# Dividing a third product of each channel group into quarters in a float32 hybrid trunk kernel on one core

## The chip, the core and the metric

The kernel runs on one core of a Trainium2 chip. TensorE multiplies, ScalarE and VectorE cut every float32 operand into a high and a low part, GpSimd forms sums of weights, and SyncE issues most of the transfers. The metric is the time of one execution in microseconds; the median of several runs counts.

## What is computed

One layer of a trunk with two token mixers. All of it starts with one wide projection of the normalised input, 1024 tokens by 1024 channels:

```
h = rmsnorm(x, norm_g)
proj = h @ w_in
b_a, c_a, x_a, z_a, q, k, v, z_b, g_a, g_b = split(proj)
y_a = short_conv_branch(b_a, c_a, x_a, z_a, ...)      # silu(z) * B * conv3(C * x), then a projection
y_b = retention_branch(q, k, v, z_b, w_b_out)         # rotary q and k, decayed chunks, silu(z) gate
merged = sigmoid(g_a) * y_a + sigmoid(g_b) * y_b
out = rmsnorm(x + merged @ w_o, final_g)
```

The change touches only the projection `h @ w_in`, without its value columns.

## The kernel before

Every float32 product is made of three TensorE products: high by high, high by low and low by high. One 2 by 2 block product is done with seven block products instead of eight (the Winograd form of Strassen's scheme). The channels of the projection are handled in 20 **groups**, g = 0 to 19, and each group does its products in `ORDER = (1, 6, 2, 5, 7, 3, 4)`. A whole product is 24 matmuls of 512 columns (`unit`, L2625 to L2628). Groups 0, 1, 18 and 19 give gates, groups 2 to 9 feed the convolution ("conv groups"), groups 10 to 17 feed rotary q and k and the silu gates ("turn groups", since q and k are turned).

Some products are **divided** once more by the same scheme: seven quarter products of 6 matmuls with 256 columns, 42 in all, in two parts (`first_half`, `second_half`, L2549 to L2551). Before the change that is product 4 in groups 1 to 18 (`TWICE`) and product 3 in groups 2 to 9 (`THIRDS`). A divided product needs quarter sums of its tokens' side (T1 to T4, in `hx` for product 4, in `third_T` for product 3), quarter sums of its weights (`second_sums`, four GpSimd additions in place, L957 to L962) and quarter additions of its results (`second_first`, L1836, and `second_rest`, three instructions at L1849), before the product's ordinary addition (`add`, L1828 and L1830).

Per unit of weights (a product, or each part of a divided one): ScalarE makes the high part (`high`, L1146), VectorE the low part (`low`, L1681, or L1678 with a changed sign), in one of three slots; slot u is free once unit u - 3 is done. Four weight buffers are loaded per group (`load_work`, roles a, b, c, d) and a fifth, e, holds the sum `s1` = b + d, which GpSimd adds (L934) for product 5. `s2` (L944) is another GpSimd addition, `s3` and `s4` are transfers that add in memory, issued by GpSimd.

Work of the group before rides along: for conv groups `conv_gate` on GpSimd, `conv_tap`, `conv_y` and `conv_early` on VectorE; for turn groups `silu` on GpSimd (L968), `turn` on VectorE (two times six steps of 512 columns, L1933 to L1947), and `turned`, which splits the turned rows (ScalarE L1318, L1319; VectorE L1954, L1956). Every engine works strictly through its own list, which the code writes out by hand; the lists meet only in semaphores. Two waits of TensorE matter here. A product may start only after VectorE added the last product that used the same banks: product 3 waits for `add` of product 5, product 4 for `add` of product 7. And the last quarter product of a divided product's second part waits for its `second_first`:

```
pe.wait_ge(sum_made, 5 * g + sums_until(ORDER, before(ORDER, product)))    # first_half; unit() alike
pe.wait_ge(value_sum, second_added(g, product, 1))                         # second_half, before T2
```

## Time and profile before

| | us |
|---|---|
| median of 3 runs | 1365.0 (1364.61 to 1365.46) |
| the profiled execution | 1365.87 |
| its span, first to last instruction | 1364.1 |
| TensorE busy in the span | 1351.8 (99%) |
| VectorE busy | 1060.0 (78%) |
| ScalarE, GpSimd busy | 608.3, 413.7 |
| one turn group | 37.6 |

The profiled execution is 0.9 us above the median, and 1.8 us of it lie outside the span. The granted clock of TensorE is 0.998 of full speed over the span. Ahead of the groups are the value columns, behind them the retention steps and the output products; neither is touched, but for the sums of product 5 in group 0.

### The profile page before, as it was taken

The page shows a single profiled execution, that of the slowest core. Times are in us where ns is not written, and L with a number is a line of the kernel's source. Part 1 is how long each engine was busy: PE and PEld are TensorE (multiplying, and loading weights), DVE is VectorE, ACT ScalarE, POOL GpSimd, SP SyncE. Part 2 cuts the span into 40 slices and gives each one's busy share as a digit, 9 for nine tenths or more (in the row PEclk, how much of TensorE's full clock was granted, in tenths as well). Part 3 has the DMA queues.
Part 4 walks back from the last instruction along what each step waited for, and adds up shares of the span by engine and source line. Part 5 has one row for each costly group of instructions (what it writes and reads, how often), then busy time and mean ns, then how long its engine had stood idle before and what let it go on. Part 6 is the DMA issues. An engine that isn't in the chain of part 4 may idle for free.

```text
span 1364.1 us, 17294 instructions
## 1 busy us (share of the span) xinstructions
PE 1351.8 (99%) x6642; PEld 1142.7 (84%) x6642; DVE 1060.0 (78%) x1097; ACT 608.3 (45%) x821; POOL 413.7 (30%) x381
## 2 busy tenths in 40 slices
PE   9999999999999999999999999999999999999997
PEld 7788888888888888888888888888888888888886
DVE  6898465677878777678888778748776998788887
ACT  6843233433333333333333433438778433433445
POOL 0100112344444554444443444315444001100002
PEclk9999999999999999999999999999999999999999
DMA  9646445344433433476666666757768699945443
GB/s 333 216 132 214 141 110 166 95 108 109 109 101 86 108 93 99 136 183 172 176 162 166 147 166 179 223 201 252 267 223 267 141 332 308 235 158 201 162 85 124
DMA packets 112979, 234.81 MB, mean 172 GB/s; under 512 B 7680, under 2 KB 50816, under 8 KB 108032
## 3 DMA queue, kind: packets, MB, share of 16 engines
q1 hardware_dynamic: 104112, 194.87, 42.2%
q0 software_dynamic: 8640, 38.80, 16.0%
q8 instruction: 53, 0.87, 0.3%
q14 instruction: 30, 0.25, 0.1%
q10 hardware_dynamic: 144, 0.02, 0.0%
HBM read 169.70 MB, written 55.57 MB: 165 GB/s over the span
## 4 chain that ended last, share of the span: by engine, by line
PE 92%; ACT 2%; issue 1%; DVE 1%; DMA 1%; POOL 1%; SPq 1%; POOLq 0%; ACTq 0%; DVEq 0%
PE psum L2625 15%; PE psum L2627 15%; PE psum L2628 15%; PE psum L2768 7%; PE psum L2766 7%; PE psum L2767 7%; PE psum L2549 3%; PE psum L2551 3%; PE psum L2550 3%; PE psum L2538 3%; PE psum L2540 3%; PE psum L2541 3%; PE psum L2670 2%; PE psum L2672 2%; PE psum L2671 2%
## 5 line engine op out<-in xcount | busy, mean ns | idle before, releaser
L1146 ACT ACTIVATE slots<-work 128x1024 fp32r<-128x1024 f32 (+1 forms) x166 | 169.5, 1027 | 418.0 <-PE psum L2628 292.1
L2625 PE MATMUL psum<-hc,slots 128*128 128x512 f32 x912 | 355.0, 389 | 0.0
L2627 PE MATMUL psum<-hc,slots 128*128 128x512 f32 x912 | 354.9, 389 | 0.0
L2628 PE MATMUL psum<-hc,slots 128*128 128x512 f32 x912 | 354.8, 389 | 0.0
L2628 PEld LDWEIGHTS psum<-hc,slots 128*128 128x128 f32 x912 | 171.2, 188 | 35.8
L2625 PEld LDWEIGHTS psum<-hc,slots 128*128 128x128 f32 x912 | 171.2, 188 | 35.3 <-issue 0.4
L2627 PEld LDWEIGHTS psum<-hc,slots 128*128 128x128 f32 x912 | 171.2, 188 | 34.8
L1435 ACT ACTIVATE last_slot<-arena 128x1024 fp32r<-128x1024 f32 x112 | 118.6, 1062 | 163.0 <-PE psum L2768 157.3
L2766 PE MATMUL psum<-last_slot 128*128 128x512 f32 (+1 forms) x452 | 175.3, 388 | 0.0
L2768 PE MATMUL psum<-last_slot 128*128 128x512 f32 (+1 forms) x452 | 175.0, 387 | 0.0
L2767 PE MATMUL psum<-last_slot 128*128 128x512 f32 (+1 forms) x452 | 175.0, 387 | 0.0
L2008 DVE TENSOR_TENSOR last_slot<-arena,last_slot 128x1024 fp32r<-128x1024 f32 x112 | 135.7, 1221 | 31.1 <-ACT last_slot L1435 30.4
L1681 DVE TENSOR_TENSOR slots<-work,slots 128x1024 fp32r<-128x1024 f32 x100 | 142.9, 1429 | 12.9 <-ACT slots L1146 12.7
L2767 PEld LDWEIGHTS psum<-last_slot 128*128 128x128 f32 x452 | 84.9, 188 | 17.4
L2766 PEld LDWEIGHTS psum<-last_slot 128*128 128x128 f32 x452 | 84.9, 188 | 17.4
L2768 PEld LDWEIGHTS psum<-last_slot 128*128 128x128 f32 x452 | 84.9, 188 | 17.2
L957 POOL TENSOR_TENSOR work<-work 128x256 f32<-128x256 f32 x26 | 23.4, 898 | 244.5 <-DVE slots L1678 244.5
L1828 DVE TENSOR_TENSOR tp_v<-psum,tp_first 128x1024 f32<-128x1024 f32 x40 | 48.8, 1220 | 55.5 <-PE psum L2628 55.3
L1678 DVE SCALAR_TENSOR_TENSOR slots<-work,slots 128x1024 fp32r<-128x1024 f32 (+1 forms) x66 | 74.8, 1133 | 20.9 <-ACT slots L1146 20.9
L2538 PE MATMUL psum<-slots,hc 128*128 128x512 f32 x224 | 88.3, 394 | 1.6 <-DVE slots L1681 1.6
L2541 PE MATMUL psum<-slots,hc 128*128 128x512 f32 x224 | 87.2, 389 | 0.0
L2540 PE MATMUL psum<-slots,hc 128*128 128x512 f32 x224 | 87.1, 389 | 0.0
(228 smaller groups left out, 2496.1 us busy)
## 6 DMA issues: line engine op xcount, KB each, us to landing
work<-w_channel SPq DMA_DIRECT2D x80, 512.0 KB, 4.0
work<-w_channel POOLq DMA_DIRECT2D x40, 512.0 KB, 5.5
arena<-w_last SPq DMA_DIRECT2D x19, 1024.0 KB, 7.9
qk<-qk_scratch SPq DMA_DIRECT2D x32, 512.0 KB, 3.4
arena<-w_last POOLq DMA_DIRECT2D x9, 1024.0 KB, 10.5
v_raw<-value_scratch SPq DMA_DIRECT2D x32, 256.0 KB, 3.9
arena<-gate_scratch SPq DMA_DIRECT2D x16, 512.0 KB, 6.8
value_c<-w_value SPq DMA_DIRECT2D x10, 512.0 KB, 4.8
```

The source lines that it names most:

```text
L1146: nc.scalar.activation(slots[:, u % SLOTS, 0, 0:columns_of(u)], src, ACT.Copy, scale=-1.0 if negated(u) else 1.0).then_inc(w_hi, 1)
L1681: nc.vector.tensor_tensor(slot[:, 1, :], src, slot[:, 0, :].bitcast(F32), ALU.subtract).then_inc(w_ready, 1)
L2008: nc.vector.tensor_tensor(slot[:, 1, :, :], pair_at(group, product, j), slot[:, 0, :, :].bitcast(F32), ALU.subtract).then_inc(last_ready, 1)
L2538: nc.tensor.matmul(bank, x_high, w_high, start=product in starts and i == 0 and kk == 0, stop=False, skip_group_check=True)
L2540: nc.tensor.matmul(bank, x_high, w_low, start=False, stop=False, skip_group_check=True)
L2541: last = nc.tensor.matmul(bank, x_low, w_high, start=False, stop=i == 1 and kk == 1, skip_group_check=True)
L2625: nc.tensor.matmul(bank, slot[:, 0, w], x_high, start=product in STARTS and j == 0, stop=False, skip_group_check=True)
L2627: nc.tensor.matmul(bank, slot[:, 0, w], x_low, start=False, stop=False, skip_group_check=True)
L2628: last = nc.tensor.matmul(bank, slot[:, 1, w], x_high, start=False, stop=j == 3, skip_group_check=True)
L2766: nc.tensor.matmul(bank, l_high, r_high, start=start, stop=False, skip_group_check=True)
L2767: nc.tensor.matmul(bank, l_high, r_low, start=False, stop=False, skip_group_check=True)
L2768: return nc.tensor.matmul(bank, l_low, r_high, start=False, stop=stop, skip_group_check=True)
```

## The change

Product 5 is divided too, in groups 2 to 17 (`FIFTHS`). What belongs to it:

- One more unit per group (`FIFTH_HALF`), so two parts for ScalarE and VectorE to make instead of one; `second_sums(g, 5)` on GpSimd; `second_first` and `second_rest` of product 5 on VectorE.
- `hx` has room for one product's T sums only. Both products' sums now lie in memory (`hx_d`), and `load_hx` brings 1.5 MB into `hx` twice in each of these groups, for 5 and for 4.
- The buffer e can no longer take its sum from b + d in place of a load. It is loaded like the others (512 KB), and `s1` becomes an adding transfer issued by GpSimd, another 512 KB; the GpSimd addition at L934 falls away in all groups but the first.
- The T sums of product 5 are made in group 0 (four quarters, four sums, four high and four low parts); those of product 4 move back to make room, and the last low parts of product 3's sums move behind the addition of product 5 in group 2.
- Order on VectorE: product 5's `second_first` comes ahead of the low part of product 7, the rest of `second_rest` is split around the next low part, and in turn groups the steps of `turn` are spread anew, with `turned` one or two units later. On GpSimd `second_sums(g, 5)` comes ahead of `conv_gate(g - 1, 2)`.

```diff
+FIFTHS = range(2, GROUPS - 2)
 def second_sums(g, product):
-            w = work[ROLES[g]["d" if product == 4 else "a"]]
+            w = work[ROLES[g][{3: "a", 4: "d", 5: "e"}[product]]]
...
         def s1(g):
+            if g:
+                work_loaded(g, "e")
+                pool.dma_start(work[ROLES[g]["e"]][:, :], w_channel[g, 2], accum_op=ALU.add).then_inc(s1_in, 16)
...
             if conv:
                 conv_gate(g - 1, 1)
                 conv_gate(g - 1, 0)
-                conv_gate(g - 1, 2)
             if turned:
                 silu(g - 1, 2)
             if turned:
                 silu(g - 1, 3)
+            if g in FIFTHS:
+                second_sums(g, 5)
+            if conv:
+                conv_gate(g - 1, 2)
...
+        def load_hx(product):
+            n = int(product == 5)
+            sp.dma_start(hx[:, 2].bitcast(F32), hx_d[n, :, 2]).then_inc(t4_in, 16)
+            sp.dma_start(hx[:, 0:2].bitcast(F32), hx_d[n, :, 0:2]).then_inc(t1_t2_in, 16)
...
+            if g in FIFTHS:
+                sp.wait_ge(unit_done, ended_at(g - 1) + 1)
+                load_hx(5)
...
+                if g in FIFTHS:
+                    sp.wait_ge(unit_done, fifth_ended_at(g) + 1)
+                    load_hx(4)
...
+                elif n == 3 and halved_product(g, 5):
+                    second_first(g, 5)
+                elif n == FIFTH_HALF:
+                    second_rest(g, 5, range(1))
+                    low(u + 2)
+                    second_rest(g, 5, range(1, 3))
+                    add(g, 5)
...
-            if g == THIRDS.start and p == 3:
-                for name in ("T2", "T4", "T3"):
+            if g == THIRDS.start and p == 4:
+                for name in ("T2", "T4", "T3", "T1"):
                     third_low(name)
-            if g == THIRDS.start and p == 4:
-                third_low("T1")
...
-                    for step in {0: (0,), 2: (1, 2, 3, 4, 5)}.get(p, ()):
+                    for step in ({0: (0,), 1: (1, 2, 3, 4), 2: (5,)} if g in FIFTHS else {0: (0,), 2: (1, 2, 3, 4, 5)}).get(p, ()):
                         turn(last, 0, step)
-                    if p == 3:
+                    if p == (FIFTH_HALF if g in FIFTHS else 3):
                         turned(last, 0)
-                    for step in {3: (0, 1, 2, 3), 4: (4, 5)}.get(p, ()):
+                    for step in ({2: (0, 1), 4: (2, 3, 4, 5)} if g in FIFTHS else {3: (0, 1, 2, 3), 4: (4, 5)}).get(p, ()):
                         turn(last, 1, step)
-                    if p == 4:
+                    if p == (5 if g in FIFTHS else 4):
                         turned(last, 1)
...
                 if halved_product(g, product):
                     first_half(g, product)
+                    if product == 5:
+                        second_half(g, 5)
```

VectorE's list in the first half of a turn group, of before; `slots` rows are low parts, `psum` rows additions, the rows with `rope_sb` and `turn_` the steps of `turn`:

```order
L1933 TENSOR_TENSOR turn_a0_88<-tp_first1_77,rope_sb_87 128x512
L1681 TENSOR_TENSOR slots_53<-work4_75,slots_53 128x1024
L1828 TENSOR_TENSOR tp_v0_78<-psum,tp_first0_76 128x1024
L1681 TENSOR_TENSOR slots_53<-work1_72,slots_53 128x1024
L1936 TENSOR_TENSOR tp_first1_77<-tp_first1_77,rope_sb_87 128x512
L1938 TENSOR_TENSOR turn_b0_90<-tp_v21_81,rope_sb_87 128x512
L1941 TENSOR_TENSOR tp_first1_77<-tp_first1_77,turn_b0_90 128x512
L1944 TENSOR_TENSOR turn_b0_90<-tp_v21_81,rope_sb_87 128x512
L1947 TENSOR_TENSOR turn_a0_88<-turn_a0_88,turn_b0_90 128x512
L1678 SCALAR_TENSOR_TENSOR slots_53<-work0_71,slots_53 128x1024
L1954 TENSOR_TENSOR tp_first1_77<-tp_first1_77,tp_v21_81 128x512
L1956 TENSOR_TENSOR turn_a0_88<-turn_a0_88,turn_b0_90 128x512
```

The same place in the changed kernel (`work4` is the buffer e, the source of product 5):

```order
L2033 TENSOR_TENSOR turn_a0_90<-tp_first1_79,rope_sb_89 128x512
L1767 TENSOR_TENSOR slots_53<-work4_77,slots_53 128x768
L2036 TENSOR_TENSOR tp_first1_79<-tp_first1_79,rope_sb_89 128x512
L2038 TENSOR_TENSOR turn_b0_92<-tp_v21_83,rope_sb_89 128x512
L2041 TENSOR_TENSOR tp_first1_79<-tp_first1_79,turn_b0_92 128x512
L2044 TENSOR_TENSOR turn_b0_92<-tp_v21_83,rope_sb_89 128x512
L1914 TENSOR_TENSOR tp_v0_80<-psum,tp_first0_78 128x1024
L1767 TENSOR_TENSOR slots_53<-work4_77,slots_53 128x1024
L2047 TENSOR_TENSOR turn_a0_90<-turn_a0_90,turn_b0_92 128x512
L2033 TENSOR_TENSOR turn_a1_91<-tp_c111_85,rope_sb_89 128x512
L2036 TENSOR_TENSOR tp_c111_85<-tp_c111_85,rope_sb_89 128x512
L1922 TENSOR_TENSOR tp_first0_78<-tp_first0_78,psum 128x256
```

Four `turn` steps moved ahead of the addition of product 6, and a second low part for product 5 and its `second_first` came in. The end of the same group on VectorE, from the addition of product 5 to the `second_first` of product 4, of before:

```order
L1828 TENSOR_TENSOR tp_v20_80<-psum,tp_first0_76 128x1024
L1678 SCALAR_TENSOR_TENSOR slots_53<-work3_74,slots_53 128x768
L1944 TENSOR_TENSOR turn_b1_91<-tp_v1_79,rope_sb_87 128x512
L1947 TENSOR_TENSOR turn_a1_89<-turn_a1_89,turn_b1_91 128x512
L1954 TENSOR_TENSOR tp_c111_83<-tp_c111_83,tp_v1_79 128x512
L1956 TENSOR_TENSOR turn_a1_89<-turn_a1_89,turn_b1_91 128x512
L1830 TENSOR_TENSOR tp_v20_80<-tp_v20_80,psum 128x1024
L1678 SCALAR_TENSOR_TENSOR slots_53<-work3_74,slots_53 128x1024
L1830 TENSOR_TENSOR tp_first0_76<-tp_first0_76,psum 128x1024
L1681 TENSOR_TENSOR slots_53<-work2_73,slots_53 128x1024
L1836 TENSOR_TENSOR tp_v0_78<-tp_v0_78,psum 128x256
```

And of the changed kernel:

```order
L1914 TENSOR_TENSOR tp_v20_82<-psum,tp_first0_78 128x1024
L2038 TENSOR_TENSOR turn_b1_93<-tp_v1_81,rope_sb_89 128x512
L2041 TENSOR_TENSOR tp_c111_85<-tp_c111_85,turn_b1_93 128x512
L2044 TENSOR_TENSOR turn_b1_93<-tp_v1_81,rope_sb_89 128x512
L2047 TENSOR_TENSOR turn_a1_91<-turn_a1_91,turn_b1_93 128x512
L1916 TENSOR_TENSOR tp_v20_82<-tp_v20_82,psum 128x1024
L1764 SCALAR_TENSOR_TENSOR slots_53<-work3_76,slots_53 128x1024
L2054 TENSOR_TENSOR tp_c111_85<-tp_c111_85,tp_v1_81 128x512
L2056 TENSOR_TENSOR turn_a1_91<-turn_a1_91,turn_b1_93 128x512
L1916 TENSOR_TENSOR tp_first0_78<-tp_first0_78,psum 128x1024
L1767 TENSOR_TENSOR slots_53<-work2_75,slots_53 128x1024
L1922 TENSOR_TENSOR tp_v0_80<-tp_v0_80,psum 128x256
```

Two more `turn` steps now stand between the additions of products 5 and 7, and `turned` stands behind the last low part of product 4. GpSimd's list of a turn group in the changed kernel, from its third `silu` to its `s2` (`work4` sums are product 5's, `work3` sums product 4's):

```order
L1040 TENSOR_TENSOR tp_first0_78<-tp_first0_78,silu_sig_94 128x512
L1040 TENSOR_TENSOR tp_v0_80<-tp_v0_80,silu_sig_94 128x512
L1029 TENSOR_TENSOR work4_77<-work4_77 128x256
L1030 TENSOR_TENSOR work4_77<-work4_77 128x256
L1032 TENSOR_TENSOR work4_77<-work4_77 128x256
L1034 TENSOR_TENSOR work4_77<-work4_77 128x256
L1029 TENSOR_TENSOR work3_76<-work3_76 128x256
L1030 TENSOR_TENSOR work3_76<-work3_76 128x256
L1032 TENSOR_TENSOR work3_76<-work3_76 128x256
L1034 TENSOR_TENSOR work3_76<-work3_76 128x256
L1040 TENSOR_TENSOR tp_c111_85<-tp_c111_85,silu_sig_94 128x512
L996 DMA work4_77<-w_channel 128x1024
```

Before, the four `work4` sums were not there, and in place of the transfer stood the addition of s1.

## Rows read from the trace of the kernel before

**Rows 1.** The page: span and busy time of the engines.

```profile
span 1364.1 us, 17294 instructions
PE 1351.8 (99%) x6642; PEld 1142.7 (84%) x6642; DVE 1060.0 (78%) x1097; ACT 608.3 (45%) x821; POOL 413.7 (30%) x381
```

**Rows 2.** Timeline of TensorE, group 12: first matmuls of products 1, 3, 4, next 1.

```profile
611.22 0.39 PE L2625 MATMUL psum<-hc,slots 128*128 128x512 f32 x1
...
638.44 0.39 PE L2625 MATMUL psum<-hc,slots 128*128 128x512 f32 x1
...
643.88 0.28 PE L2549 MATMUL psum<-hc,slots 128*128 128x256 f32 x1
...
648.81 0.39 PE L2625 MATMUL psum<-hc,slots 128*128 128x512 f32 x1
```

**Rows 3.** Stretches (conv, turn): busy PE, PEld, DVE, ACT, POOL; clock, DMA share, GB/s.

```profile
350.00:387.00 37.00, 37.00 (x205) 32.30 (x204) 28.95 (x28) 12.78 (x14) 17.34 (x16) 1.00 0.39 101
649.00:686.60 37.60, 37.60 (x187) 31.96 (x186) 30.67 (x34) 14.27 (x18) 16.67 (x13) 1.00 0.64 167
```

**Rows 4.** Timeline of VectorE, turn group 12; start, length, idle before in brackets.

```profile
613.74 1.22 DVE L1681 TENSOR_TENSOR slots<-work,slots 128x1024 fp32r<-128x1024 f32 x1
614.87 1.22 DVE L1830 TENSOR_TENSOR tp_v<-tp_v,psum 128x1024 f32<-128x1024 f32 x1
616.00 2.62 DVE L1681 TENSOR_TENSOR slots<-work,slots 128x1024 fp32r<-128x1024 f32 x1
618.55 0.68 DVE L1933 TENSOR_TENSOR turn_a<-tp_first,rope_sb 128x512 f32<-128x512 f32 x1
...
622.32 1.22 DVE L1828 TENSOR_TENSOR tp_v<-psum,tp_first 128x1024 f32<-128x1024 f32 x1 [1.96 <-PE psum L2628]
...
638.38 1.15 DVE L1954 TENSOR_TENSOR tp_c<-tp_c,tp_v 128x512 fp32r<-128x512 f32 x1 [0.70 <-ACT tp_v L1318]
...
646.54 0.41 DVE L1836 TENSOR_TENSOR tp_v<-tp_v,psum 128x256 f32<-128x256 f32 x1
...
649.01 2.40 DVE L1849 TENSOR_TENSOR tp_v<-tp_v,psum 128x768 f32<-128x768 f32 x3 [2.06 <-PE psum L2551]
```

**Rows 5.** Timeline of GpSimd, the same group.

```profile
615.95 1.58 POOL L968 TENSOR_TENSOR tp_first<-tp_first,silu_sig 128x512 f32<-128x512 f32 x1
...
619.44 2.06 POOL L968 TENSOR_TENSOR tp_v<-tp_v,silu_sig 128x512 f32<-128x512 f32 x1 [1.91 <-ACT silu_sig L1297]
...
637.09 1.20 POOL L958 TENSOR_TENSOR work<-work 128x256 f32<-128x256 f32 x1
638.25 0.74 POOL L960 TENSOR_TENSOR work<-work 128x256 f32<-128x256 f32 x1
...
649.06 1.34 POOL L968 TENSOR_TENSOR tp_v<-tp_v,silu_sig 128x512 f32<-128x512 f32 x1
```

**Rows 6.** Timeline of ScalarE, the same group: a high part, `turned`, PSUM copy.

```profile
627.75 1.06 ACT L1146 ACTIVATE slots<-work 128x1024 fp32r<-128x1024 f32 x1 [4.38 <-PE psum L2628]
...
628.72 0.61 ACT L1318 ACTIVATE tp_v<-tp_first 128x512 fp32r<-128x512 f32 x1
...
629.76 1.01 ACT L1278 ACTIVATE tp_c<-psum 128x1024 f32<-128x1024 f32 x1
```

**Rows 7.** Timeline of VectorE, conv group 4: the end of its riding work.

```profile
328.39 1.23 DVE L1916 TENSOR_TENSOR taps<-taps,gate_z 128x1024 f32<-128x1024 f32 x1
...
334.94 1.22 DVE L1828 TENSOR_TENSOR tp_v<-psum,tp_first 128x1024 f32<-128x1024 f32 x1 [2.72 <-PE psum L2628]
```

**Rows 8.** The page: queues, and issues with the time to landing.

```profile
q1 hardware_dynamic: 104112, 194.87, 42.2%
q0 software_dynamic: 8640, 38.80, 16.0%
work<-w_channel POOLq DMA_DIRECT2D x40, 512.0 KB, 5.5
```

**Rows 9.** Timeline of VectorE, group 2: low parts of product 3's sums.

```profile
256.58 1.83 DVE L1882 TENSOR_TENSOR third_T<-t_sums,third_T 128x512 fp32r<-128x512 f32 x2
```

More of the change, by code:

```diff
@@ L342, in build @@
     t4_sums = sb("t4_sums", CONS_AT + 8 * KB, [P, 4, 2, QUARTER])
+    t5_high, t5_low = (sb(f"t5_{n}", TP_AT[1] + m * 8 * KB, [P, 4, 2, QUARTER]) for m, n in enumerate(("high", "low")))
     t3_quarters = sb("t3_quarters", CONS_AT, [P, 4, 2, QUARTER])
@@ L2111, in _ @@
                     low(u + 1)
+                    low(u + 2)
+            elif u >= VALUE_UNITS and place_of(u)[0] in FIFTHS and place_of(u)[1] in (0, 1, 2, 3, 4, FIFTH_HALF):
+                conv = place_of(u)[0] - 1 in CONVS
+                if place_of(u)[1] == 0 or place_of(u)[1] in (1, 2) and not conv:
+                    low(u + 2)
+                if place_of(u)[1] == 0 and conv:
+                    low(u + 3)
+                if place_of(u)[1] == FIFTH_HALF:
+                    low(u + 1)
+                    if place_of(u)[0] in CONVS:
+                        conv_early(place_of(u)[0])
                     low(u + 2)
@@ L2172, in _ @@
             if kind_of(g) == "conv":
-                if p == 3:
+                if p == 3 and g not in FIFTHS:
                     conv_early(g)
@@ L2592, in unit @@
                 pe.wait_ge(kept_in, 80)
+            if product == 5 and g == FIFTHS.stop:
+                pe.wait_ge(fifth_kept, 192)
             if product == 3 and g == THIRDS.stop:
```

194 lines of the change are left out of this document (136 added, 58 removed).

## The prediction

> **What bounds the kernel now.** I read the page first. TensorE is busy for 99% of the span [rows 1], so in the groups a saved matmul is saved time as long as nobody else is late. Then I read the timeline of TensorE in one turn group for the spacing of its matmuls: product 3, whole, takes from 638.44 to 643.88 = 5.44 us for 24 matmuls, product 4, divided, from there to 648.81 = 4.93 us for 42; the group takes 648.81 - 611.22 = 37.59 us [rows 2]. Then I read who is next. Busy time by stretch says VectorE: 28.95 of 37.0 us in a conv group, 30.67 of 37.6 us in a turn group, with the queues at 0.39 and 0.64 of their time [rows 3]. So the change takes from the engine that is full and gives to one with about 7 us left per turn group.
>
> **What the division saves.** 5.44 - 4.93 = 0.51 us a group [rows 2], in 16 groups 8.2 us. The Trainium skill (TensorE: Matmul & The Clock Gate, Back-to-back issue gap) spaces single warm matmuls at N / 2.4 + 2.5 ns; by that a whole product would be 24 x 215.8 = 5.18 us, a divided one 42 x 109.2 = 4.59 us, and the saving 0.59 us a group or 9.5 us in all. The rows give 0.51, and the sum goes by them.
>
> **How VectorE and GpSimd hinder each other.** This decides the rest. The low part at 616.00 lasts 2.62 us where the one at 613.74 lasts 1.22: it ends at 618.62, 1.09 us after the `silu` of GpSimd that began at 615.95 and lasted 1.58 [rows 4, 5]. The `silu` at 619.44 lasts 2.06 where the one at 649.06, beside a VectorE instruction that reads PSUM, lasts 1.34. At 637.09 and 638.38 they take turns: a quarter sum 1.20 (alone 0.74), a 512-column step 1.15 (alone 0.68). So an instruction of VectorE with both inputs in SBUF and one of GpSimd never run together, and when both are ready they alternate; additions from PSUM are free of it. In such turns I charge 0.55 us for a step, 0.60 for a quarter sum, 1.18 for a `silu` (each duration less its share of waiting). Started back to back, VectorE's low parts follow at 1.13 us (613.74 to 614.87), short ones (768 columns) at an estimated 0.87, steps at 0.60 or, where one needs the one before, 0.72.
>
> **A turn group, walked.** Clock zero is the end of the group before (611.4 in group 12); TensorE without any stall would end product 6 at 10.9, 2 at 16.3, 5 at 18.5 (first part) and 21.3, 7 at 26.7, 3 at 32.1, 4 at 34.3 (first part) and 37.1; the next product's first matmul starts 0.16 before each. I follow VectorE's new list.
> - Until 7.2 it is the old one: it reaches the first `turn` step at 618.55 [rows 4]. The step runs to 7.8, the short low part of product 5 to 8.7. The last `silu`, ready since about 7.9, now takes its turn to 9.8.
> - The four `turn` steps that were moved here then meet the four new quarter sums, which may start once that low part is made. They alternate: steps until 13.8, sums until 14.4, where four steps alone take 2.8 us. Before, VectorE was idle for 1.96 us at this place [rows 4].
> - Addition of product 6 until 15.0 (due at 16.2). The second part of product 5 needs all four sums: ScalarE's high part 14.5 to 15.6, low part to 16.8 (due 18.3). Three steps to 18.7, `second_first` to 19.1, low part of product 7 to 20.2 (due 21.1). ScalarE gets to product 3's high part only after the one of product 7, two copies for `turned` and the PSUM copy: 3.0 us from the start of the first to the end of the last [rows 6], then 1.0 more, so from 16.4 and a wait for the steps to 20.5; low part to 21.7, `turned` to 22.9.
> - `second_rest` and the low part between: the three at 649.01 last 2.40 together; 22.9 to 26.0. Addition of product 5 to 27.3. **Product 3 should have started at 26.55 and waits for it: about 0.8 us.** Before, this addition had the 5.44 us of product 7 almost to itself.
> - Four steps meet the last of product 4's sums and a `silu`, to 31.4. Addition of 7 to 32.5, low part of 4's second part to 33.7, `turned` to 34.9, addition of 3 to 36.0, low part of the next group to 37.2, `second_first` of 4 to 37.5. TensorE's last quarter product wanted it at 36.2. **The delay is now 1.3 us in all**, of which 0.8 is the first, and the group ends at about 38.4.
> So a turn group takes 38.4 where it took 37.6: +0.8. In the old order the same last instruction starts at 646.54 and is wanted at 648.1 (six matmuls, 0.7 us, ahead of 648.81), and VectorE is idle for 2.06 us behind it [rows 2, 4]: that slack is what is spent. The next group starts with GpSimd's `s2` some 1.1 us later than before, which costs nothing yet: the low part that needs it stands behind `second_rest` until 2.4. I add 0.1 for a late restart. This holds for groups 11 to 17, whose predecessor is a turn group: 7 x 0.9 = **+6.3**.
>
> **A conv group, walked.** The tap and its product with the gate ended at 328.39 + 1.23 = 16.5 after the group's start [rows 7]; now the low part in between and the quarter sums put this at 18.8. ScalarE's copy into `u_pad` waits for it, then the gate's sigmoid, then product 3's high part (20.7), low part 21.7; `second_rest` and a low part that meets product 3's quarter sums, to 25.3; addition of 5 to 26.6 against 26.55 wanted. That is a stall of 0.1 to 0.2 (before, the addition that stands there had idle time of 2.72 us ahead of it). `conv_early` ends at 20.9, wanted at 21.1. Further, `s1` is now an adding transfer issued at about 28.3 and s2 wants it at 33.9; such transfers land 5.5 us after issue [rows 8], so 33.8: it may push the next group by some tenths. I take -0.51 + 0.3 = -0.2 each for groups 3 to 9: **-1.4**. Bounds: -0.5 if nothing is late, +0.5 if the transfer lands 1 us late.
>
> **Group 10** has the conv work but no division of 3: **-0.5**. **Group 2**: the four low parts of product 3's sums (two at 256.58 in 1.83, where two alone would take 1.3, since they take turns with quarter sums [rows 9]) now start only behind the addition of product 5, at about 25.8, and the last waits for ScalarE in between: done at 29 to 30, where product 3 wants them at 26.55. 3.0 us of stall less 0.5: **+2.5** (bounds +1.0 and +3.5).
>
> **What I cost at nothing.** Group 0's new sums (16 short instructions of 0.6 to 0.7 us on VectorE) fit in, since no group work rides there; without that cover they would cost up to 10 us once. The loads of `hx`: product 5's is issued at zero and wanted at 17.8, product 4's at 21.3 and wanted at 30 (conv) or 34; 1.5 MB at q1's rate, 194.87 MB in 42.2% of 1364 us = 339 GB/s, is 4.6 us [rows 8]. On SyncE, behind them wait only loads whose own condition comes later.
>
> **Sum.** 6.3 - 1.4 - 0.5 + 2.5 = +6.9 us. The profiled execution, 1365.87, would become 1372.8; it stands 0.9 above the median, so the median of the changed kernel is 1365.0 + 6.9 = 1372.
>
> **The rivals.**
> - *VectorE keeps up* (faster). Should the `silu` and the quarter sums fall into gaps instead of alternating with the steps (place: 7.9 to 14.4), the list is 2.4 us shorter and no turn group waits. Then 16 x 0.51 = 8.2 is gained, group 2 loses 3.0: 1360, or 1357 if that too is hidden. It decides when the list is 0.8 us shorter than I walked it. For it: my rows are of one group and most of the new meetings are constructed. Against: the alternation is in the rows, and VectorE's work grows by at least 3.6 us beside it. 0.22.
> - *Both about cancel* (turn groups lose 0.2 to 0.4 each): 1363 to 1367. 0.11.
> - *The queues are full.* 3.5 MB more on q1 at 339 GB/s and 0.5 MB more on q0 (38.8 MB in 16.0%, 178 GB/s) are 10.3 + 2.9 = 13.2 us of all queues a group; a turn group has 0.64 x 37.6 = 24 already: 37.3 of 37 [rows 3, 8]. Then `s1` lands late everywhere, some 1 us more in 14 groups with half of it hidden: 1372 + 7 = 1379. 0.17. The Trainium skill (DMA: Bandwidth & Descriptors, the table at its head) gives about 358 GB/s from memory per core; a turn group would move 167 + 108 = 275, so by that page the queues are not full.
> - The forecast: 0.50.
>
> The range for 8 in 10 runs from 1360, the whole gain with group 2's loss, to 1381. A difference of 0.2% (2.7 us) is about what a measurement of this kernel can tell. Faster 0.22, same 0.11, slower 0.67.
>
> **What would show it.** Right: TensorE's first matmul of product 3 waits for the addition of product 5 in groups 11 to 17, and its last quarter product of 4 for `second_first`; turn groups of 38.2 to 38.7 us, VectorE busy for over 95% of them; in group 2 a stall of 2 us or more at product 3; no wait of TensorE for `hx`. Wrong: turn groups of 37.1 us, or idle time of VectorE left ahead of product 5's `second_rest`; GpSimd's sums unlengthened at 10 to 14 us of a turn group.

## The result, and the profile after

| | before | after |
|---|---|---|
| median | 1364.8 (6 runs, 1364.1 to 1365.5) | 1376.1 (6 runs, 1372.7 to 1377.6) |
| span of the profiled execution | 1364.1 | 1374.1 |
| groups 3 to 9, each | 37.18 | 36.92 (group 5: 37.68) |
| group 10 | 37.60 | 37.11 |
| groups 11 to 17, each | 37.59 | 38.43 to 38.56, group 12 39.25, group 17 39.58 |
| group 2 | 37.48 | 41.86 |

The ratio is 1.008, 95% interval 1.0069 to 1.0092: 0.8% slower. A group's length is read from the end of the last matmul of one group to that of the next. By groups the spans differ by +4.37 us (group 2), -1.05 (groups 3 to 9), -0.49 (group 10), +8.15 (11 to 17) and -0.91 (the value columns ahead of the groups): +10.07 together. The medians differ by 11.3, since the profiled execution of the kernel before stands 1.1 above its median and that of the changed one 0.2 below.

The page of the changed kernel: busy times (answers to [rows 1]), TensorE's whole matmuls with the idle time ahead of them, the two queues and the adding transfers [rows 8].

```profile
PE 1351.4 (98%) x6930; PEld 1151.6 (84%) x6930; DVE 1125.0 (82%) x1189; ACT 623.1 (45%) x841; POOL 445.3 (32%) x445
...
L2760 PE MATMUL psum<-hc,slots 128*128 128x512 f32 x784 | 306.0, 390 | 6.7 <-DVE tp_v L1914 6.7
...
q1 hardware_dynamic: 118928, 260.41, 54.3%
q0 software_dynamic: 11376, 48.76, 18.8%
...
work<-w_channel POOLq DMA_DIRECT2D x59, 512.0 KB, 8.0
```

TensorE's busy time hardly fell, although its matmuls need 8 us less: busy time also counts a matmul that is held up, as at the halved clock below, where a 256-column matmul counts 0.41 us instead of 0.28. VectorE's busy time grew by 65 us. What TensorE waited for, the changed kernel (total, times, longest):

```profile
PE psum L2760 <- DVE tp_v L1914: 6.7, 7, 1.5
PE psum L2676 <- DVE third_T L1982: 3.4, 1, 3.4
...
PE psum L2676 <- DMA hx<-hx_scratch: 0.7, 1, 0.7
```

The first line is product 3 waiting for the addition of product 5, once in each turn group from 11 on; the second is product 3 of group 2 waiting for its own low parts; the third, in group 5, is a load of T sums that landed late. The stretches that answer to [rows 3], a conv group and turn group 14:

```profile
316.30:353.30 37.00, 37.00 (x224) 33.06 (x223) 31.24 (x34) 13.48 (x16) 20.67 (x19) 1.00 0.72 215
691.90:730.30 38.40, 37.58 (x205) 32.32 (x204) 36.06 (x38) 15.11 (x19) 18.56 (x17) 1.00 0.92 275
```

VectorE was busy for 30.67 of 37.6 us of a turn group and is now for 36.06 of 38.4. The share of the queues went from 0.64 to 0.92. VectorE's timeline in group 14, at the places of the walk:

```profile
700.46 1.77 DVE L2036 TENSOR_TENSOR tp_first<-tp_first,rope_sb 128x512 f32<-128x512 f32 x1
702.15 1.22 DVE L2038 TENSOR_TENSOR turn_b<-tp_v,rope_sb 128x512 f32<-128x512 f32 x1
703.41 1.11 DVE L2041 TENSOR_TENSOR tp_first<-tp_first,turn_b 128x512 f32<-128x512 f32 x1
704.55 1.11 DVE L2044 TENSOR_TENSOR turn_b<-tp_v,rope_sb 128x512 f32<-128x512 f32 x1
705.59 1.21 DVE L1914 TENSOR_TENSOR tp_v<-psum,tp_first 128x1024 f32<-128x1024 f32 x1
707.44 1.23 DVE L1767 TENSOR_TENSOR slots<-work,slots 128x1024 fp32r<-128x1024 f32 x1 [0.65 <-ACT slots L1223]
...
717.94 1.23 DVE L1914 TENSOR_TENSOR tp_v<-psum,tp_first 128x1024 f32<-128x1024 f32 x1
```

GpSimd beside it, and TensorE's first matmul of product 3:

```profile
701.64 1.19 POOL L1029 TENSOR_TENSOR work<-work 128x256 f32<-128x256 f32 x1
...
719.31 0.47 PE L2760 MATMUL psum<-hc,slots 128*128 128x512 f32 x1 [0.73 <-DVE tp_v L1914]
```

Four steps of `turn` and the quarter sums alternate as walked (1.11 to 1.77 us a step where one alone takes 0.68, 1.19 a sum where one alone takes 0.74). The addition of product 5 (the second L1914) ends at 719.17, and product 3 starts behind it, 0.9 us later than its spacing would have it. The Trainium skill (SBUF — State Buffer, Who interferes with whom) says that a VectorE instruction with two SBUF inputs contends with a GpSimd instruction that reads SBUF; the trace agrees, with L1914, which reads PSUM, at its 1.21 us beside the last sum.

In group 2 the wait has a sequel. Timeline of VectorE, then of TensorE, then stretches (granted clock is the third number from the end):

```profile
263.38 1.93 DVE L1982 TENSOR_TENSOR third_T<-t_sums,third_T 128x512 fp32r<-128x512 f32 x2
265.24 1.21 DVE L1982 TENSOR_TENSOR hc<-t_sums,hc 128x512 fp32r<-128x512 f32 x1
266.37 1.21 DVE L1982 TENSOR_TENSOR third_T<-t_sums,third_T 128x512 fp32r<-128x512 f32 x1
```

```profile
267.72 0.52 PE L2676 MATMUL psum<-hc,slots 128*128 128x256 f32 x1 [3.45 <-DVE third_T L1982]
```

```profile
264.00:267.70 3.70, 0.27 (x2) 0.01 (x1) 3.70 (x5) 1.21 (x2) 3.62 (x5) 1.00 0.31 128
267.70:269.50 1.80, 1.78 (x8) 1.80 (x9) 1.80 (x2) 0.47 (x1) 1.04 (x2) 0.52 0.46 59
269.50:271.10 1.60, 1.60 (x10) 1.60 (x9) 0.34 (x1) 0.00 (x0) 0.00 (x0) 0.50 1.05 187
271.10:273.00 1.90, 1.90 (x17) 1.90 (x17) 0.42 (x1) 1.06 (x1) 0.00 (x0) 0.98 1.05 209
```

```profile
268.26 0.36 PE L2676 MATMUL psum<-hc,slots 128*128 128x256 f32 x1 [3.44 <-DVE third_T L1982]
...
264.50:268.20 3.70, 0.32 (x2) 0.00 (x0) 3.70 (x5) 1.17 (x2) 3.62 (x5) 1.00 0.00 0
268.20:270.00 1.80, 1.74 (x14) 1.77 (x15) 1.80 (x2) 0.51 (x1) 1.08 (x2) 1.00 0.54 48
```

### The profile page after: what moved, and what is told of

The parts are those of the page before. It is cut to its first block, busy times and chain, and to the rows that moved or that the text cites. A ratio compares the mean times of both kernels' runs of the same rounds, so it can differ in the third digit from the quotient of the medians.

```text
span 1374.1 us, 18228 instructions
## 1 busy us (share of the span) xinstructions
PE 1351.4 (98%) x6930; PEld 1151.6 (84%) x6930; DVE 1125.0 (82%) x1189; ACT 623.1 (45%) x841; POOL 445.3 (32%) x445
## 4 chain that ended last, share of the span: by engine, by line
PE 74%; DVE 10%; ACT 4%; POOL 3%; issue 3%; DMA 3%; SPq 2%; POOLq 0%; DVEq 0%; ACTq 0%
PE psum L2760 9%; PE psum L2762 9%; PE psum L2763 9%; PE psum L2905 7%; PE psum L2903 7%; PE psum L2904 7%; PE psum L2676 4%; PE psum L2678 3%; PE psum L2677 3%; PE psum L2665 3%; PE psum L2667 3%; PE psum L2668 3%; PE psum L2805 2%; PE psum L2807 2%; PE psum L2806 2%
## 5 line engine op out<-in xcount | busy, mean ns | idle before, releaser
L1223 ACT ACTIVATE slots<-work 128x1024 fp32r<-128x1024 f32 (+1 forms) x182 | 181.7, 1009 | 394.3 <-POOL work L1034 160.4
L2760 PE MATMUL psum<-hc,slots 128*128 128x512 f32 x784 | 306.0, 390 | 6.7 <-DVE tp_v L1914 6.7
L2762 PE MATMUL psum<-hc,slots 128*128 128x512 f32 x784 | 305.3, 389 | 0.0
L2763 PE MATMUL psum<-hc,slots 128*128 128x512 f32 x784 | 305.2, 389 | 0.0
L1767 DVE TENSOR_TENSOR slots<-work,slots 128x1024 fp32r<-128x1024 f32 x116 | 157.1, 1360 | 28.1 <-ACT slots L1223 28.1
L2760 PEld LDWEIGHTS psum<-hc,slots 128*128 128x128 f32 x784 | 147.2, 188 | 38.8 <-issue 9.5
L2763 PEld LDWEIGHTS psum<-hc,slots 128*128 128x128 f32 x784 | 147.1, 188 | 31.0
L2762 PEld LDWEIGHTS psum<-hc,slots 128*128 128x128 f32 x784 | 147.2, 188 | 29.1
L1029 POOL TENSOR_TENSOR work<-work 128x256 f32<-128x256 f32 x42 | 37.8, 901 | 189.1 <-DVE slots L1764 176.7
L2676 PE MATMUL psum<-hc,slots 128*128 128x256 f32 x336 | 95.3, 284 | 3.4 <-DVE third_T L1982 3.4
L2678 PE MATMUL psum<-hc,slots 128*128 128x256 f32 x336 | 95.4, 284 | 0.0
L2677 PE MATMUL psum<-hc,slots 128*128 128x256 f32 x336 | 95.2, 283 | 0.0
L2665 PE MATMUL psum<-slots,hc 128*128 128x512 f32 x224 | 88.3, 394 | 0.6 <-DVE slots L1767 0.6
```

The lines of the kernel that those rows point to most:

```text
L1223: nc.scalar.activation(slots[:, u % SLOTS, 0, 0:columns_of(u)], src, ACT.Copy, scale=-1.0 if negated(u) else 1.0).then_inc(w_hi, 1)
L1767: nc.vector.tensor_tensor(slot[:, 1, :], src, slot[:, 0, :].bitcast(F32), ALU.subtract).then_inc(w_ready, 1)
L2676: nc.tensor.matmul(to, slot[:, 0, w], high, start=start and j == 0, stop=False, skip_group_check=True)
L2677: nc.tensor.matmul(to, slot[:, 0, w], low, start=False, stop=False, skip_group_check=True)
L2678: last = nc.tensor.matmul(to, slot[:, 1, w], high, start=False, stop=j == 1, skip_group_check=True)
L2760: nc.tensor.matmul(bank, slot[:, 0, w], x_high, start=product in STARTS and j == 0, stop=False, skip_group_check=True)
```

## The experiments

Ratios and medians are against the kernel before, in runs on the same chip (1364.9 to 1365.1). Where a range is given, the median is of 4 to 11 executions; otherwise there is one. "Takes" of a product means from the end of the one before to its own end; without a wait a whole product takes 5.44 us, the two parts of a divided one 2.13 and 2.80.

### Group 2's low parts earlier

```diff
-            if g == THIRDS.start and p == 4:
-                for name in ("T2", "T4", "T3", "T1"):
+            if g == THIRDS.start and p == 3:
+                for name in ("T2", "T4", "T3"):
                     third_low(name)
+            if g == THIRDS.start and p == FIFTH_HALF:
+                third_low("T1")
```

> The changed kernel with the last low parts of product 3's sums in group 2 made earlier: three at product 5's first part, the fourth (and its high part) at its second part. Theory 1 (they are what product 3 waited for, and the half clock behind that wait is its consequence): group 2 falls from 41.9 us to 37.2 or less, the clock stays at full speed there, the kernel gains 4.6 to 5.0 us against the changed one, 1371 to 1372 us. Theory 2 (the addition of product 5 is late there anyway, for its own reasons): product 3 still waits 1 us or more, the gain is under 3 us.

1371.7 (1370.0 to 1373.9), ratio 1.005 [1.0034, 1.0067]. Group 2 takes 37.18 instead of 41.86, with the granted clock at 1.00. The low parts take 0.69 each again, the first of them:

```profile
250.92 0.69 DVE L1982 TENSOR_TENSOR third_T<-t_sums,third_T 128x512 fp32r<-128x512 f32 x1
```

So 4.7 us of that group hung on the place of four short instructions, the halved clock with them. The median fell by 4.4. Product 3 of group 2 still takes 0.5 us too long, and product 7 of groups 3 and 4 now takes 0.5 and 0.2 more than in the changed kernel; why is told below, with product 5 divided in groups 2 to 10 alone.

### What the alternation with the quarter sums costs

```diff
+            n_columns = 8 if product == 5 and g > QZS.start else QUARTER
-            a11, a12, a22, a21 = (w[:, n * QUARTER:(n + 1) * QUARTER] for n in range(4))
+            a11, a12, a22, a21 = (w[:, n * QUARTER:n * QUARTER + n_columns] for n in range(4))
```

> The changed kernel, but product 5's four quarter sums on GpSimd take 8 columns instead of 256 in groups 11 to 17 (the output is not the reference's there). The prediction's rival had it that without the turns with these sums VectorE's list is 2.4 us shorter and no turn group waits: turn groups of 37.1 us. The other theory: the list has to wait at product 3's low part for ScalarE, whose high part stands behind the two copies of turned, so most of the 2.4 us becomes idle time and the turn groups fall only from 38.45 to about 38.2 us.

The sums of product 5 cover only 8 of 256 columns here, so that product is wrong; what is asked is the time. 1373.9 (span 1372.1). Turn groups take 38.32 to 38.35, but for group 12 (39.34): 0.1 less than with the whole sums. In group 14 three of the four steps run alone (0.68 to 0.74 us) and the list gets 2 us ahead. Then it waits for TensorE, ahead of `second_first` of product 5:

```profile
710.06 0.42 DVE L1923 TENSOR_TENSOR tp_first<-tp_first,psum 128x256 f32<-128x256 f32 x1 [1.82 <-PE psum L2679]
```

and for 0.3 us more for ScalarE's high part of product 3. The alternation is real and was nearly free.

### A shorter `second_rest`

```diff
+                n_columns = 8 if product == 5 and g > QZS.start else QUARTER
-                at = to[:, quarters, :]
+                at = to[:, quarters, 0:n_columns]
```

> The changed kernel, but the three quarter additions of product 5 behind its second part (second_rest) take 8 columns per quarter in groups 11 to 17 (the output is not the reference's). They stand behind the place where VectorE meets ScalarE, so if VectorE's list from there on is what delays TensorE, the 1.8 us taken out count in full: the wait of 0.85 us for the addition of product 5 and that of 0.25 us behind it are gone, turn groups of 37.1 to 37.3 us. If the queues or GpSimd set the pace, they stay near 38.4 us.

Three additions of VectorE cover 8 columns of each 256 in these groups and take 1.8 us less together; product 5 is wrong here too. 1371.4 (span 1369.6). Product 3's wait is gone (5.44), but the group takes 37.8 to 38.2 (17: 39.0). TensorE's waits name the place:

```profile
PE psum L2677 <- DVE tp_v L1922: 2.7, 7, 0.4
```

Product 4's last quarter product waits for `second_first`, so that its second part takes 3.45 us instead of 2.80, and its first part takes up to 0.3 more. Of the 1.8 us taken from the list only 0.3 to 0.7 arrived (1.4 in group 12): three waits stand one behind the other.

### Shorter loads of the T sums

```diff
-            sp.dma_start(hx[:, 2].bitcast(F32), hx_d[n, :, 2]).then_inc(t4_in, 16)
-            sp.dma_start(hx[:, 0:2].bitcast(F32), hx_d[n, :, 0:2]).then_inc(t1_t2_in, 16)
+            sp.dma_start(hx[:, 2, 0, 0].bitcast(F32), hx_d[n, :, 2, 0, 0]).then_inc(t4_in, 16)
+            sp.dma_start(hx[:, 0, 0, 0].bitcast(F32), hx_d[n, :, 0, 0, 0]).then_inc(t1_t2_in, 16)
```

> The changed kernel, but each of the two loads of hx brings one row of 512 bytes per partition instead of 4 or 8 KB, so 3 MB a group are not moved (the products read stale sums, the output is not the reference's). Theory vector list: turn groups 11, 13 to 16 stay at 38.4 to 38.5 us, and only what came on top, 0.8 us in group 12, 1.1 us in group 17 and 0.8 us in group 5, goes away: 2.5 to 3 us in all. Theory full queues: all turn groups fall below 38 us and the kernel gains 5 us or more.

The products with `hx` read sums that are mostly not loaded here, so they are wrong. 1373.1 (span 1371.2). Turn groups 38.43 to 38.48, one of them (14) 39.27; group 5 36.92. Without nearly 3 MB of loads a group the common turn group is as long as with them, so these loads do not make the 38.4. That they made the longer groups isn't shown: with the whole loads, the next kernel has none of 5, 12 and 17 either (36.93, 38.32, 38.29), and group 14 is long here without them, its `s2` held up by the adding transfer of `s1` until 2.0 us after the group's start instead of 1.2. Of the 2.9 us that the span fell, 1.5 are the half clock that is absent in group 2.

### The turned low parts later still

```diff
-                    if p == (FIFTH_HALF if g in FIFTHS else 3):
+                    if p == (4 if g in FIFTHS else 3):
                         turned(last, 0)
```

and the same on ScalarE.

> Only one thing differs from the changed kernel: in groups 11 to 17 the two turned low parts (0.7 us each on VectorE) and their ScalarE parts stand one step later, behind the addition of product 5 instead of ahead of it. Theory 1 (VectorE's list is what product 3 waits for): that addition ends about 1.2 to 1.4 us earlier, the wait of 0.9 us at product 3 is gone, and product 3 takes 5.44; but the list is as long as it was, so the first added part of product 4 comes late in its place: its last quarter product, 3.04 to 3.05 now, goes to 3.3 to 3.5, as with the shortened last parts of product 5. A group takes 37.8 to 38.1 instead of 38.4 to 38.6, the whole 1371 to 1373. Theory 2 (TensorE waits in these groups for the queues, whose transfers are late): moving two additions of VectorE changes nothing, 38.4 and more stay. Theory 3 (the turned parts are themselves late for products 1 and 6 of the next group): product 1 or 6 grows instead by what product 3 gives back.

1373.4 (span 1371.6). Product 3 takes 5.44, and product 4 waits instead: its first part takes 2.68 or more instead of 2.13, its second 3.44. Turn groups take 38.27 to 38.57. The wait moved almost whole, not only into the last quarter product:

```profile
PE psum L2676 <- DVE tp_v L1916: 2.8, 7, 0.6
PE psum L2676 <- DVE tp_v L1922: 2.7, 7, 0.4
```

The first line is the addition of product 7 (L1916), now behind `turned` as well. I had expected 37.8 to 38.1. (Group 2 is 0.9 us longer here: its half clock lasted 6.8 us.)

### The tail turned round

```diff
+                if n == 6 and g in QZS:
+                    second_first(g, 4)
+                    low(u + 1)
+                    add(g, 3)
```

in place of `add` of 3, the low part, `second_first` of 4. The turned low parts stand later as in the kernel before this one.

> The turned parts later as in the kernel before this one, and VectorE's order at the end of groups 11 to 17 turned round: the first added part of product 4 first, then the low part of the next group's first product, then the addition of product 3. Theory 1 (two waits of TensorE on an engine that still has some 1 us a group of its own idle time): VectorE is busy 36.1 us of a group and waits 0.9 to 1.0 for ScalarE and TensorE, so both waits of TensorE go away and a group takes 37.1 to 37.3, which is the length of its matmuls; the whole 1364 to 1367 with group 2 unmended. Theory 2 (the list has no room left: VectorE is the bound of the group): the wait moves to another product and the group stays at 37.8 or more, the whole at 1369 or more.

1371.6 (1369.9 to 1372.9), ratio 1.0048 [1.0033, 1.0064]. The second part of product 4 takes 2.80 again; its first part takes 2.8 to 3.2, waiting for the addition of product 7, which the edit did not touch. Groups 37.8 to 38.4, one 38.9. Theory 1's 37.1 was wrong: there were three waits in line and I had mended two.

### Product 5 divided in groups 2 to 10 alone

```diff
-FIFTHS = range(2, GROUPS - 2)
+FIFTHS = range(2, 11)
```

with group 2's low parts earlier.

> Product 5 divided in groups 2 to 10 alone, with the low parts of group 2's last sums made two steps earlier. Theory 1 (the loss is group 2's wait and the turn groups; the rest gains): groups 3 to 9 take 36.9 each against 37.2 of the kernel before, group 10 37.1 against 37.6, group 2 37.2 against 37.5, groups 11 to 17 the 37.6 of before: 1364.8 less 1.8, 0.5 and 0.3 is 1362.2, with a late transfer or two up to 1363.5. That is faster than both kernels by more than a measurement's doubt. Theory 2 (a divided product costs its group something that only shows later, in the queues): the groups behind the divided ones lengthen by tenths, and the whole stays at 1364.5 or more.

1363.7 (11 runs, 1362.2 to 1365.4), ratio 0.9992 [0.9983, 1.0000]. Groups 4, 5, 7 and 9 take 36.93, group 10 37.11, group 2 37.16, groups 11 to 17 37.59. In groups 3, 6 and 8 product 7 takes 0.1 to 0.9 us more, 1.4 in all. The sum of parts holds; the median gain of 1.1 us is less than the 2.6 that the undisturbed groups would give. The profile names no releaser for this wait ("issue"), but the kernel does: product 7 waits for `conv_early` (L1994) to have read the banks of product 2.

```
            elif prior == 2:
                pe.wait_ge(c11_read, g + 1)
```

Group 6, which starts at 385.75; GpSimd's `s2`, VectorE's `conv_early`, TensorE's product 7:

```profile
384.01 2.41 POOL L1016 TENSOR_TENSOR work<-work,work 128x1024 f32<-128x1024 f32 x1 [4.96 <-DMA work<-w_channel]
...
406.84 0.68 DVE L1994 TENSOR_TENSOR gate_z<-psum,gate_z 128x512 f32<-128x512 f32 x1
...
407.62 0.47 PE L2762 MATMUL psum<-hc,slots 128*128 128x512 f32 x1 [0.59 <-issue]
```

TensorE starts 0.1 us behind `conv_early`; in the groups without this wait it starts 0.23 behind it. `conv_early` is late because VectorE's list is, from the low part that needs `s2` on, and `s2` because the adding transfer of `s1` took 6.7 us to land instead of 5.5. Twelve of the kept traces (all but those of the kernel before and of the last experiment) have GpSimd's order of this kernel there, with 84 conv groups (3 to 9) in all. In the 72 of them where `s2` ends 0.2 us or more ahead of the group's start, product 7 takes 5.45 or 5.46. In the other 12 it takes more, and the more the later: 5.50 at -0.12, 5.73 at 0.08, 5.92 at 0.28, 6.31 at 0.67.

### All three orders mended

This joins the three edits (group 2, turned parts, tail), with product 5 divided in groups 2 to 17.

> Product 5 divided in groups 2 to 17, the low parts of group 2's last sums earlier, the turned parts later and VectorE's order at the end of groups 11 to 17 turned round. Theory 1 (all three losses are orders of VectorE's list): groups 3 to 9 take 36.9, group 10 37.1, group 2 37.2, groups 11 to 17 37.1 to 37.3 each, the whole 1359 to 1361, with late transfers in three or four groups up to 1364. Theory 2 (VectorE's list is full in groups 11 to 17): these stay at 37.8 or more, the whole at 1365 or more, slower than with product 5 divided in groups 2 to 10 alone. Theory 3 (the queues are next): most groups reach 37.2, but transfers that land late, as in groups 12 and 17 of the changed kernel, cost more than 3 us in all, the whole 1363 to 1366.

1366.8 (11 runs, 1365.9 to 1369.4), ratio 1.0015 [1.0006, 1.0024]. Turn groups 37.9 to 38.3, one 38.5. Group 14 on VectorE:

```profile
712.74 1.78 DVE L2056 TENSOR_TENSOR turn_a<-turn_a,turn_b 128x512 fp32r<-128x512 f32 x1
714.44 0.68 DVE L2038 TENSOR_TENSOR turn_b<-tp_v,rope_sb 128x512 f32<-128x512 f32 x1
...
716.60 0.69 DVE L2047 TENSOR_TENSOR turn_a<-turn_a,turn_b 128x512 f32<-128x512 f32 x1
717.21 1.21 DVE L1916 TENSOR_TENSOR tp_v<-tp_v,psum 128x1024 f32<-128x1024 f32 x1
```

The addition of product 7 could run from 712.5 and stands behind four steps that nobody waits for.

### The addition of product 7 ahead of the steps

```diff
                 elif ORDER[n] not in (1, 2):
                     add(g, ORDER[n])
+                    if ORDER[n] == 7 and g in FIFTHS and kind_of(g - 1) == "turn":
+                        for step in (2, 3, 4, 5):
+                            turn(g - 1, 1, step)
```

with these steps taken out at their old place.

> As the kernel with all three orders mended, and in groups 11 to 17 one more order of VectorE: the addition of product 7 stands ahead of the last four steps of the second turn (4 x 0.69 us) and not behind them. In the kernel with all mended, product 4's first half waits 0.8 to 1.0 us for this addition, which starts at 717.2 in group 14, while product 7 has ended at 712.5. Theory 1 (this wait too is one of order: of a group of 37.97 VectorE is busy 36.4): the addition starts at 714.4, the wait is gone, the low part behind it stands where it stood, and a group takes 37.2 to 37.4, the whole 1362 to 1364. Theory 2 (VectorE's list, with 0.65 us of waiting for ScalarE in it and what it loses while GpSimd works, is as long as the group): the wait moves on again, to the first added part or to the next group's products, and a group stays at 37.8 to 38.0, the whole at 1366 or more.

1364.8 (11 runs, 1363.4 to 1366.7), ratio 0.9998 [0.9989, 1.0007]: level with the kernel before. Product 4's waits are gone (2.13 and 2.83). Group 11 takes 37.09, which is the length of its matmuls; the others 37.5 to 37.8 with some tenths each at the first part of product 5, at 7 and at 3; group 13 takes 39.87, since TensorE waits 2.09 us there at the first part of product 5. VectorE and ScalarE in group 13:

```profile
656.38 0.69 DVE L2033 TENSOR_TENSOR turn_a<-tp_first,rope_sb 128x512 f32<-128x512 f32 x1 [2.35 <-DMA qk_scratch<-turn_a]
...
654.91 1.03 ACT L1344 ACTIVATE tp_first<-psum 128x1024 f32<-128x1024 f32 x1 [2.64 <-DMA qk_scratch<-tp_c]
```

Both engines wait for the stores of the turned rows to be over, in a stretch where the queues have no time left (share 1.06):

```profile
650.00:655.00 5.00, 5.00 (x24) 4.14 (x23) 4.03 (x3) 1.58 (x4) 2.22 (x2) 1.00 1.06 268
```

Seven groups show such a wait on ScalarE, five on VectorE, 4.9 and 3.2 us in all.

### Is the list the bound once the orders are mended?

The shorter `second_rest` and the shorter quarter sums from above, on the kernel with all three orders mended, one execution each.

> As the kernel with all three orders mended, and in groups 11 to 17 the last parts of product 5's addition on 8 columns of each 256, so product 5 isn't completely added; this takes some 2.1 us from VectorE's list of a group. Theory 1 (the length of VectorE's list is the bound of these groups, by some 0.8 us): TensorE waits for nothing in them, a group takes 37.1, the length of its matmuls, and the whole some 1359 to 1361. Theory 2 (something else, a slot or a transfer, has taken over at 37.9): the groups stay at 37.7 or more.

> As the kernel with all three orders mended, and in groups 11 to 17 GpSimd makes the quarter sums of product 5 on 8 columns of 256, so product 5's divided sums are wrong. It takes 4.2 us of GpSimd's work away from beside VectorE's turn steps (two of these take 1.11 beside it and 0.69 alone) and lets ScalarE's high part of product 5 come some 3 us earlier, for which VectorE's list waits 0.65. Theory 1 (the list is the bound now, so what lengthens it shows in full): a group falls by 0.6 to 0.9, to 37.1 to 37.4, though the same edit gave only 0.1 while product 3 waited. Theory 2 (the alternation is as harmless as it was before): it falls by 0.1 again, to 37.8 or more.

With the shorter `second_rest` 1363.3 (span 1361.5), turn groups 37.39 to 37.43, two of 37.84 and 37.87. With the small sums 1365.4 (span 1363.6), 37.65 in six groups, 39.23 in one. So both edits count now, and the sums for more than they did while product 3 waited: the first gives 0.57 us (37.97 to 37.39 or 37.43), the second 0.32 where it was 0.1. VectorE's list sets these groups, but not alone, since neither reaches 37.1.

### Product 4's quarter sums ahead of product 3's

```diff
+            if g in TWICE:
+                second_sums(g, 4)
             if g in THIRDS:
                 second_sums(g, 3)
-            if g in TWICE:
-                second_sums(g, 4)
```

> As the kernel with product 5 divided in groups 2 to 10 alone, and in groups 2 to 9 GpSimd makes the quarter sums of product 4 ahead of those of product 3, which are multiplied last. In that kernel the last quarter product of 4 takes 3.03 to 3.07 instead of 2.80 in groups 3 to 9: its high part on ScalarE starts at 340.5 in group 4, when the sums of 4 (337.5 to 340.4) are ready behind those of 3 (333.7 to 337.5). Theory 1 (the order of the sums is the cause): the sums of 4 start when the low part of 4's first product is made, 335.4, and are ready by 338.5, 2 us earlier; the wait of 0.25 is gone, a group takes 36.7, and 7 groups give 1.7 us: the whole 1362.0 where that kernel has 1363.7, or 0.2% under the kernel before. Theory 2 (VectorE's list is the cause: between the additions and the low part it has no room there): the 0.25 stays, 36.9 a group, 1363.7. Theory 3 (the loads of s1's part and the adding transfer, issued 1 us later, are late for the next group): product 6 of the next group lengthens by tenths and takes the gain.

This is the kernel with product 5 divided in groups 2 to 10 alone, with one more order turned round. 1391.3 (1388.7 to 1392.4), ratio 1.0189 [1.0176, 1.0203]. The wait it aimed at is gone (the second part of product 4 takes 2.80 in groups 3 to 8); but a conv group takes 39.5 to 41.4, so this alone doesn't prove the cause, as other waits give the sums time there. In group 2 `s1`'s adding transfer is issued at 270.50, 30.7 us into the group, where the kernel without this edit issues it at 28.5. From there, GpSimd, then TensorE in group 3:

```profile
270.50 0.88 POOL L996 DMA_DIRECT2D work<-w_channel  x1
...
277.21 2.39 POOL L1016 TENSOR_TENSOR work<-work,work 128x1024 f32<-128x1024 f32 x1 [4.93 <-DMA work<-w_channel]
```

```profile
282.98 0.47 PE L2762 MATMUL psum<-hc,slots 128*128 128x512 f32 x1 [0.95 <-DVE slots L1767]
```

`s2` (L1016) ends at 279.60, 3.0 us after group 3's start, instead of 0.3 after. Product 6 starts 1.2 us late; products 5 and 7 each lose about 1 us more, in six of the seven groups. At product 7 of group 7 the profile itself names `conv_early`:

```profile
461.15 0.47 PE L2762 MATMUL psum<-hc,slots 128*128 128x512 f32 x1 [0.81 <-DVE gate_z L1994]
```

In the remaining one (group 8) product 6 loses 4.3: a wait of 2.40 us, and 0.9 us after its end a half clock for 3.4 us. Theory 3 was right in its mechanism and ten times too small. The chain (sums, transfer, `s2`) has two ends. At product 6 it has room: `s2` 2.77 later cost 1.2 there, so some 1.5 us were left. At product 7 it has next to none: in the kernel as changed `s2` ends 0.28 us or more ahead of the group's start, and product 7 suffers from about -0.15 on.

## Why the prediction was right

It said 1372, range 1360 to 1381, slower with 0.67; 1376.1 was measured. Point by point:

- **Saving of 0.51 per product**: right. Group 10 takes 37.11 and, with the orders mended, group 11 37.09, against 37.6.
- **Turn groups 38.4, product 3 waiting 0.8 and 1.3 in all**: 38.43 to 38.56 in five of seven, product 3 starting 0.85 to 1.0 late, the last quarter product 0.25, and some 0.1 at each restart. Shown by what moves it: without `second_rest`'s length, or with `turned` behind the addition, product 3's wait is gone. "VectorE busy for over 95%" was 94%.
- **Groups 12 and 17** took 0.8 to 1.1 more each. The walk had nothing for this. In group 12 the first step of `turn` waits for a store of the turned rows, with the queues at 1.07 in that stretch; behind it the list falls in with the `silu` and the sums at other points. In group 17 `s2` waited for `s1`'s adding transfer until the group had begun, and the low part of product 6 came 1 us late. Which groups are hit differs between executions, with the whole loads and with the shorter ones. This is the third rival in small: the queues are full at the head of a group, not over the whole of it (0.92 to 0.94, 275 GB/s). The two rows, VectorE in group 12 and GpSimd in 17:

```profile
622.05 0.69 DVE L2033 TENSOR_TENSOR turn_a<-tp_first,rope_sb 128x512 f32<-128x512 f32 x1 [0.71 <-DMA qk_scratch<-turn_a]
...
807.29 2.41 POOL L1016 TENSOR_TENSOR work<-work,work 128x1024 f32<-128x1024 f32 x1 [7.27 <-DMA work<-w_channel]
```

- **Conv groups -0.2**: -0.26 in six of seven, though not by the stall that I named: the number was right in part by luck. Product 3 starts in time; it is the second part of product 4 that takes 0.24 more, at its start. In group 4 the last of the eight quarter sums ends at 344.84 and ScalarE's high part starts at 344.93, so it waits for them; the last experiment agrees. "It may push the next group by some tenths", said of s1's transfer: not in the change as made, but by up to 0.9 us in 12 conv groups of the kernels tried, at product 7, and by microseconds when it goes 2 us later. `conv_early`, which I had ending at 20.9, ends there and is the gate.
- **Group 2, +2.5 (bounds +1.0 and +3.5)**: the term that was mis-sized; it measured +4.4. The wait was 3.6 where I had 3.0 (done at 30.0 of my "29 to 30"), because two more low parts alternated with quarter sums (1.21 each), and the halved clock behind it, some 1.5 us, was in no bound. The 0.3 us that product 7 of this group lost in the kernel before fell away.
- **The rival "VectorE keeps up"** said the list would be 2.4 us shorter without the alternation "and no turn group waits". The small sums refute its second half: 38.33. The list has later gates, TensorE's first quarter products of product 5's second part and ScalarE's high part of product 3.
- **No wait of TensorE for `hx`**: one, of 0.7 us in group 5. What I cost at nothing in group 0 did cost nothing: 38.24 before and after.

Sum in the prediction's terms: turn groups +8.15 for +6.3 (1.9 of it in groups 12 and 17), conv and group 10 -1.54 for -1.9, group 2 +4.37 for +2.5, and -0.91 from the value columns, which the change doesn't touch and whose difference stays unexplained: +10.07 for +6.9.

As for a version that beats both kernels: product 5 divided in groups 2 to 10 alone has a median 1.1 us under the kernel before (0.9992, interval up to 1.0000), within the 0.2% that a measurement can tell; it is 0.9% under the change. Dividing it in the turn groups as well, with four orders mended, comes level (0.9998). Open stays whether an earlier issue of `s1`'s transfer would free product 7 of the conv groups, and earlier stores of the turned rows the heads of the turn groups; neither was tried.

## What to carry to other kernels

When work moves from a full engine to one with 18% of its time left, walk that engine's whole list in order: the idle time is usable only up to each gate, and several waits stand in line, so that mending one uncovers the next (0.9 us at product 3, then 0.6 at product 4's first part, then 0.65 at its last, and only with all three mended did the group fall from 38.4 to between 37.5 and 37.8 in five of seven, and to 37.1 in one). A long single wait of TensorE can cost more than its length: five of six did, by 1.5 us or more. Before moving work ahead on the engine that issues an adding transfer, measure how much that transfer has left at every instruction that hangs on it: here some 1.5 us at product 6 but 0.1 to 0.3 at product 7, and an issue 2.2 us later went past both and, repeated in every conv group, cost 1.9%. And where a profile names no releaser for a wait, look up what the kernel waits for there, and compare its distance in the groups with and without the wait.

## What the runs showed of the hardware

- After 3.45 us without a matmul, with the granted clock still shown as 1.00 in that stretch, TensorE ran at 0.50 to 0.52 for 3.4 us and then at full clock. The same wait was followed by half clock for 3.4 us in three more executions and for 6.8 us in one, and by none in one (1.00 throughout). A wait of 2.40 us was followed by it once. The waits of 0.7 to 2.1 us left the clock at 1.00. The Trainium skill (TensorE: Matmul & The Clock Gate, Part 1: The HAM clock gate) says that a hardware block sets the array's clock by how busy it has been recently; the granted clock agrees in that, within the groups, it fell only behind such waits, and the execution at 1.00 shows that a wait of this length doesn't settle it.
- An adding transfer took 8.0 us from issue to landing (median of 59) where it took 5.5 [rows 8], at a queue share that rose from 0.64 to 0.92 in the turn groups. That of `s1` alone took 5.5 to 5.7 us into groups 3 to 10 and 7.0 to 9.0 into the turn groups 11 to 17.
- A DMA share above 1 (1.06 to 1.12) marks the head of a turn group. There even stores, which nothing seems to need soon, held up VectorE by 2.35 us and ScalarE by 2.64, since the next group writes the buffers that they read.
